# Seven half products for eight in eight pairs of projection blocks, with sums on VectorE and GpSimd and another step order

## What is computed

```python
proj = x @ w_in[l]
aq, ak, av, dqkv, dbeta, da, dz, gates = jnp.split(proj, SPLIT_POINTS, axis=-1)
...
dqkv = jax.nn.silu(causal_depthwise_conv(dqkv, conv_w[l]))
...
g = -jnp.exp(a_log[l].astype(jnp.float32)) * jax.nn.softplus(da.astype(jnp.float32) + dt_bias[l].astype(jnp.float32))
...
x = layer_norm(DEEPNORM_ALPHA * x + merged @ w_out[l], ln1_g[l], ln1_b[l])
h = jnp.square(jax.nn.relu(x @ w_up[l]))
x = layer_norm(DEEPNORM_ALPHA * x + h @ w_down[l], ln2_g[l], ln2_b[l])
```

## Time and profile before

| | us |
|---|---|
| median of 3 runs | 1449.0 |
| lowest, highest | 1446.56, 1449.88 |
| the profiled execution | 1448.78 |
| its span, as the profile has it | 1446.7 |
| TensorE busy | 1423.5 |
| VectorE busy | 893.3 |
| ScalarE busy | 525.6 |
| GpSimd busy | 316.0 |
| mean granted clock of TensorE | 0.996 of 2.4 GHz |

### The profile page before, as it was taken

One profiled execution on the slowest core, in us unless ns is written; L12 is line 12 of the kernel. 1 busy time (PEld: TensorE's weight loads), 2 busy tenths in 40 slices (PEclk: granted clock), 3 DMA queues, 4 the chain that ended last, 5 costly groups with the idle time before them and its releaser, 6 DMA issues.

```text
span 1446.7 us, 22466 instructions
## 1 busy us (share of the span) xinstructions
PE 1423.5 (98%) x8570; PEld 1173.8 (81%) x8570; DVE 893.3 (62%) x1710; ACT 525.6 (36%) x1182; POOL 316.0 (22%) x341
## 2 busy tenths in 40 slices
PE   8999999999999999999999999999999999999996
PEld 7888887888888888778888888888888788888885
DVE  3555323565656665455518798666764777777778
ACT  3221212333323333252302435555554544444540
POOL 3666534242422333133740000000000000000000
PEclk9999999999999999999999999999999999999998
DMA  6222524423443233134451234333444865555422
GB/s 221 73 87 101 167 97 129 122 73 98 125 110 109 72 107 89 63 107 148 172 206 58 88 131 166 139 140 146 160 161 165 330 215 185 165 169 182 127 70 117
DMA packets 114703, 194.92 MB, mean 135 GB/s; under 512 B 27760, under 2 KB 60592, under 8 KB 112304
## 3 DMA queue, kind: packets, MB, share of 16 engines
q1 hardware_dynamic: 105680, 174.21, 36.5%
q10 hardware_dynamic: 8928, 19.40, 3.6%
HBM read 135.84 MB, written 57.74 MB: 134 GB/s over the span
## 4 chain that ended last, share of the span: by engine, by line
PE 93%; DVE 4%; ACT 1%; DMA 1%; issue 0%; SPq 0%; ACTq 0%; DVEq 0%
PE ps L1819 15%; PE ps L1753 10%; PE ps L1754 10%; PE ps L1755 10%; PE ps L2189 6%; PE ps L2190 6%; PE ps L2191 6%; PE ps L2173 5%; PE ps L2172 5%; PE ps L2174 5%; PE ps L1887 4%; PE ps L1827 2%; PE ps L1968 1%; PE ps L1919 1%; PE ps L1765 1%; PE ps L1947 1%
## 5 line engine op out<-in xcount | busy, mean ns | idle before, releaser
L716 POOL TENSOR_TENSOR ring2l<-raw,ring2h 128x256 fp32r<-128x256 f32 x180 | 175.2, 1004 | 3.6
L2189 PE MATMUL ps<-thi,shi 128*128 128x512 f32 x416 | 162.5, 391 | 2.6 <-DVE tlow L1642 2.6
L2190 PE MATMUL ps<-tlow,shi 128*128 128x512 f32 x416 | 162.6, 391 | 0.0
L2191 PE MATMUL ps<-thi,slow 128*128 128x512 f32 x416 | 162.4, 390 | 0.0
L1819 PE MATMUL ps<-xh,ring2h 128*128 128x512 f32 x304 | 122.4, 403 | 0.0
L1819 PE MATMUL ps<-xl,ring2h 128*128 128x512 f32 x304 | 122.2, 402 | 0.0
L1819 PE MATMUL ps<-xh,ring2l 128*128 128x512 f32 x304 | 120.4, 396 | 0.0
L713 POOL CAST ring2h<-raw 128x1024 fp32r<-128x1024 f32 x45 | 48.8, 1085 | 322.5 <-PE ps L1819 177.2
L1753 PE MATMUL ps<-xh,ring2h 128*128 128x512 f32 x288 | 112.2, 390 | 0.0
L1754 PE MATMUL ps<-xl,ring2h 128*128 128x512 f32 x288 | 112.1, 389 | 0.0
L1755 PE MATMUL ps<-xh,ring2l 128*128 128x512 f32 x288 | 112.1, 389 | 0.0
(11 more groups left out here) (348 smaller groups left out, 3229.2 us busy)
## 6 DMA issues: line engine op xcount, KB each, us to landing
raw<-in_wblk SPq DMA_DIRECT2D x55, 512.0 KB, 3.3
sraw<-hpark SPq DMA_DIRECT2D x104, 256.0 KB, 2.8
hpark<-hq SPq DMA_DIRECT2D x16, 1024.0 KB, 4.6
b<-in_wblk SPq DMA_DIRECT2D x64, 256.0 KB, 3.5
wraw<-in_wblk SPq DMA_DIRECT2D x30, 512.0 KB, 4.0
park<-ub ACTq DMA_DIRECT2D x50, 256.0 KB, 2.0
hpark<-hq SPq DMA_DIRECT2D x16, 768.0 KB, 5.0
park<-cout ACTq DMA_DIRECT2D x12, 512.0 KB, 2.6
```

The lines of the kernel that those rows point to most:

```text
L716: ins = pool.tensor_tensor(lo[:, k:k + 2, :], src[:, k:k + 2, :], hi[:, k:k + 2, :].bitcast(F32), ALU.subtract)
L2189: mm(outp, shi[s][:, ts], thi[m][:, :], start=first, stop=False, skip_group_check=True)
L2190: mm(outp, shi[s][:, ts], tlow[m][:, :], start=False, stop=False, skip_group_check=True)
L2191: return mm(outp, slow[s][:, ts], thi[m][:, :], start=False, stop=final, skip_group_check=True)
```

## The change

Block 0 is now the first query block, and the 12 DeltaNet blocks are 1 to 12. Block 0 is projected as before. Blocks 1 to 16 are done as eight pairs: a pair (256 columns) and x are cut in quarters, A by rows of w and block, B by rows of w and token half. `in7` does seven products of half depth and 512 tokens, in the order P1, P5, P6, P2, P7, P3, P4, 12 matmuls each. P1, P6, P7 and P4 share one bank, P5 and P3 another, P2 has a third; between products ScalarE copies the bank's present state to cb (`in_snap`), and VectorE adds banks to these copies (`combine_in`). Two sets of four banks alternate.

- Four sums of x, T1 to T4, are made once, by VectorE, from the raw x, split by ScalarE and VectorE, and stored over the raw x and above.
- Four sums of weights for a pair, S1, S2, S4 and S3, are made by GpSimd (`in_sums`). High parts of the seven pieces are made by ScalarE (`in_hi`), low parts by VectorE (`in_lo`). Each piece has one buffer (A22 has two), so each waits for its product of the pair before.
- SP loads the two blocks of pair n when the raw data of pair n - 1 are used up: four sums and five low parts, for pair 1 all seven.
- ScalarE does the first tap of the convolution. The SiLU is done in place.
- The end of the decay chain is moved behind the last combination. The gate matmuls, block 17 and the split of blocks 17 and 18 on GpSimd follow the last pair.
- In the steps the order on all three engines and the list of fillers are others: 19 places for 14. TensorE's order is now: scores, kk, kq, t1, vn of the first chunk, y1, ds, pt, u1, ks of the second chunk, pv, y2, scores, vn of the second chunk, u2, ds, grow, y3, both o, u3, y4, u4, pt and trk, trq, ont, y5, pv, u5, trv, with fillers between.
- At the seam to the down projection the parts of step 2 come before ScalarE's relus and VectorE's four sums.
- For a single tile the inverse root takes seven instructions for nine.

All waits on shared semaphores are shifted by the counts of the new part. The core of the diff (without the orders of the steps on VectorE and ScalarE, which the text above and the functions' names tell, and the buffers' addresses):

```diff
+N_IP = 8
+I_SP, I_TX, I_SN, I_CS = 7 * N_IP, 4 * N_IP, 4 * N_IP, 3 * N_IP
+IPROD = [("A11", "B11", 0), ("S1", "T1", 1), ("S2", "T2", 0), ("A12", "B21", 2), ("S3", "T3", 0), ("S4", "B22", 1), ("A22", "T4", 0)]
...
+PREP0 = ("A11", "S1", "S2", "A12", "S3", "S4", "A22")
+PREP = ("A11", "A22", "S1", "S2", "A12", "S3", "S4")
...
+            def load_in(n):
+                sp.dma_start(raw[n % 2][:, :], A["wblk"][n, :, :]).then_inc(w_raw_in[n % 2], 16)
...
+            for n in range(1, N_IP + 1):
+                sp.wait_ge(tx_sum, 4 * n)
+                sp.wait_ge(up_w, 7 * n - 2 if n > 1 else 7)
+                load_in(2 * n + 1)
+                load_in(2 * n + 2)
...
+            def in_sums(n):
+                pool.wait_ge(w_raw_in[1], 16 * (n + 1))
+                pool.wait_ge(w_raw_in[0], 16 * (n + 2))
+                own = lambda k: ipw[k][2]
+                if n:
+                    pool.wait_ge(sp_mm, 7 * (n - 1) + I_P5)
+                pool.tensor_tensor(own("S1"), IA["A21"], IA["A22"], ALU.add).then_inc(tx_sum, 1)
+                pool.wait_ge(tx_sum, 4 * n + 1)
+                if n:
+                    pool.wait_ge(sp_mm, 7 * (n - 1) + I_P6)
+                else:
+                    pool.wait_ge(av_mm, NT)
+                pool.tensor_tensor(own("S2"), own("S1"), IA["A11"], ALU.subtract).then_inc(tx_sum, 1)
+                pool.wait_ge(tx_sum, 4 * n + 2)
+                if n:
+                    pool.wait_ge(up_w, 7 * (n - 1) + ip_order(n - 1).index("S4") + 1)
+                pool.tensor_tensor(s4raw, IA["A12"], own("S2"), ALU.subtract).then_inc(tx_sum, 1)
+                if n:
+                    pool.wait_ge(sp_mm, 7 * (n - 1) + I_P7)
+                pool.tensor_tensor(own("S3"), IA["A11"], IA["A21"], ALU.subtract).then_inc(tx_sum, 1)
+            for n in range(N_IP):
+                in_sums(n)
...
+            pool.wait_ge(sp_mm, 7 * (N_IP - 1) + I_P5)
+            pool.sem_inc(w_hi, 2 * N_IP)
+            pool.sem_inc(w_ready, 2 * N_IP)
+            split(N_IP, 1, ring2h[1], ring2l[1])
+            pool.wait_ge(sp_mm, 7 * N_IP)
+            split(N_IP + 1, 0, ring2h[0], ring2l[0])
+            split_ring(N_IP + 1, 1)
...
+            def in_hi(n, *pieces):
+                for k in pieces:
+                    hi, lo, src = ip_piece(n, k)
+                    assert ip_order(n)[ic["n"] % 7] == k
+                    ic["n"] += 1
+                    if k in ("A11", "A12"):
+                        act.wait_ge(w_raw_in[1], 16 * (n + 1))
+                    elif k == "A22":
+                        act.wait_ge(w_raw_in[0], 16 * (n + 2))
+                    else:
+                        act.wait_ge(tx_sum, 4 * n + {"S1": 1, "S2": 2, "S4": 3, "S3": 4}[k])
+                    if n == 0:
+                        if k == "A12":
+                            act.wait_ge(av_mm, NT)
+                        if k in ("S4", "A22"):
+                            act.wait_ge(uni_mm, 2)
+                    elif k == "A22":
+                        if n == 1:
+                            for h in range(2):
+                                act.wait_ge(ub_out[h], 16)
+                        else:
+                            act.wait_ge(sp_mm, 7 * (n - 2) + I_P4)
+                    else:
+                        act.wait_ge(sp_mm, 7 * (n - 1) + {"A11": I_P1, "S1": I_P5, "S2": I_P6, "A12": I_P2, "S3": I_P7, "S4": I_P3}[k])
+                    cp(hi, src).then_inc(up_hi, 1)
...
+            def t_hi(i):
+                act.wait_ge(ti_sum, 3 if i < 2 else 4)
+                cp(ith[IT_ORDER[i]][:, :, :, :], itr[IT_ORDER[i]][:, :, :, :]).then_inc(xh_ok, 1)
+            def in_snap(n, i):
+                prod, bank, block, half = ((I_P1, 0, 0, 0), (I_P5, 1, 1, 1), (I_P6, 0, 0, 1), (I_P4, 0, 1, 0))[i]
+                act.wait_ge(sp_mm, 7 * n + prod)
+                if n == 0:
+                    act.wait_ge(zero_ok, 2)
+                elif n >= 2:
+                    act.wait_ge(conv_ok, 2 * (n - 2) + block + 1)
+                if i == 3:
+                    act.wait_ge(cs_ok, 3 * n + 2)
+                cp(ip_cb(n, block, half), ip_bank(n, bank)).then_inc(snap_ok, 1)
...
+            def tap0(b):
+                n, p = divmod(b, 2)
+                act.wait_ge(cs_ok, 3 * n + 3)
+                act.wait_ge(snap_ok, 4 * n + 4)
+                if b == 0:
+                    act.wait_ge(c_in, 16 * 7)
+                if b >= 2:
+                    act.wait_ge(dn_out[p], 16 * n)
+                act.activation(cacc[p][:, :], cb[2 * (n % 2) + p][:, 0:S], ACT.Identity, bias=zero[:, 0:1], scale=convw[:, b, 0:1]).then_inc(tap_ok, 1)
+            def silu_store(b):
+                p = b % 2
+                act.wait_ge(conv_ok, b + 1)
+                act.activation(cacc[p][:, :], cacc[p][:, :], ACT.Silu).then_inc(silu_ok, 1)
...
+                act.dma_start(park[b, :, PAD:PAD + S], cacc[p][:, :]).then_inc(dn_out[p], 16)
...
+            in_hi(0, "A11", "S1")
+            t_hi(0)
+            in_hi(0, "S2")
+            t_hi(1)
+            in_hi(0, "A12")
+            q_half(0)
+            t_hi(2)
+            in_hi(0, "S3")
+            t_hi(3)
+            q_half(1)
+            in_hi(0, "S4", "A22")
+            for n in range(N_IP):
+                conv = 1 <= n <= N_DN // 2
+                ahead = n < N_IP - 1
+                if n:
+                    in_snap(n - 1, 3)
+                if conv:
+                    tap0(2 * n - 2)
+                    tap0(2 * n - 1)
+                if n == N_IP - 1:
+                    store_pair(n - 1)
+                in_snap(n, 0)
+                if ahead:
+                    in_hi(n + 1, "A11", "A22")
+                in_snap(n, 1)
+                if ahead:
+                    in_hi(n + 1, "S1")
+                if conv:
+                    silu_store(2 * n - 2)
+                in_snap(n, 2)
+                if ahead:
+                    in_hi(n + 1, "S2", "A12")
+                if conv:
+                    silu_store(2 * n - 1)
+                if ahead:
+                    in_hi(n + 1, "S3", "S4")
...
+            act.wait_ge(g_raw, 1)
+            act.activation(gtmp[:, 0, :, :], ba[:, :, 0:NH], ACT.Exp, scale=-1.0)
+            act.activation(gtmp[:, 5, 0, :], alog[:, :], ACT.Exp)
+            act.activation(gtmp[:, 2, :, :], gtmp[:, 2, :, :], ACT.Exp, scale=-1.0).then_inc(g_exp, 1)
+            in_snap(N_IP - 1, 3)
+            store_pair(N_IP - 1)
...
+            def conv(b):
+                p, src = b % 2, cb[b % 4]
+                dve.wait_ge(tap_ok, b + 1)
                 for k in range(1, 4):
...
+            ic = {"n": 0}
+            def in_lo(n, *pieces):
+                for k in pieces:
+                    hi, lo, src = ip_piece(n, k)
+                    assert ip_order(n)[ic["n"] % 7] == k
+                    ic["n"] += 1
+                    dve.wait_ge(up_hi, ic["n"])
+                    if k in ("S1", "S2"):
+                        dve.wait_ge(tx_sum, 4 * n + {"S1": 2, "S2": 3}[k])
+                    tt(lo, src, hi.bitcast(F32), ALU.subtract).then_inc(up_w, 1)
+            def combine_in(n, i):
+                prod, bank, block, half, snap = ((I_P2, 2, 0, 0, 1), (I_P7, 0, 1, 1, 2), (I_P3, 1, 0, 1, 3))[i]
+                dve.wait_ge(sp_mm, 7 * n + prod)
+                dve.wait_ge(snap_ok, 4 * n + snap)
+                c = ip_cb(n, block, half)
+                tt(c, c, ip_bank(n, bank), ALU.add).then_inc(cs_ok, 1)
+            def t_lo(i):
+                dve.wait_ge(xh_ok, NT + i + 1)
+                tt(itl[IT_ORDER[i]][:, :, :, :], itr[IT_ORDER[i]][:, :, :, :], ith[IT_ORDER[i]][:, :, :, :].bitcast(F32), ALU.subtract).then_inc(xl_ok, 1)
+            ti = {k: r[:, :, :, :] for k, r in itr.items()}
+            xq = lambda kk, half: xraw[:, 4 * half:4 * half + 4, 4 * kk:4 * kk + 4, :]
+            tt(ti["T3"], xq(1, 1), xq(0, 1), ALU.subtract).then_inc(ti_sum, 1)
+            tt(ti["T1"], xq(0, 1), xq(0, 0), ALU.subtract).then_inc(ti_sum, 1)
+            in_lo(0, "A11")
+            dve.wait_ge(ti_sum, 2)
+            tt(ti["T2"], xq(1, 1), ti["T1"], ALU.subtract).then_inc(ti_sum, 1)
+            dve.wait_ge(ti_sum, 3)
+            tt(ti["T4"], xq(1, 0), ti["T2"], ALU.subtract).then_inc(ti_sum, 1)
+            in_lo(0, "S1")
+            t_lo(0)
+            in_lo(0, "S2")
+            t_lo(1)
+            in_lo(0, "A12")
+            t_lo(2)
+            in_lo(0, "S3")
+            t_lo(3)
+            in_lo(0, "S4", "A22")
+            for n in range(N_IP):
+                convs = 1 <= n <= N_DN // 2
+                ahead = n < N_IP - 1
+                if convs:
+                    conv(2 * n - 2)
+                if ahead:
+                    in_lo(n + 1, "A11", "A22", "S1")
+                if convs:
+                    conv(2 * n - 1)
+                combine_in(n, 0)
+                if ahead:
+                    in_lo(n + 1, "S2", "A12")
+                combine_in(n, 1)
```

(59 more changed lines are left out.)

302 lines of the change are left out of this document (145 added, 157 removed).

## The result

The changed kernel takes 1468.7 us (median of 4 runs, 1467.2 to 1470.4) where the kernel before takes 1449.4 beside it: ratio 1.0135, 95% interval 1.0122 to 1.0149. That is 19.3 us more; the forecast was 11.1 more. The profiled execution has a span of 1466.1 us against 1446.7.

A forecast was written before the change was run, and what follows sets the result against it. TensorE, busy 98% of the span, was taken as the bound; -21.8 + 11.6 + 16.2 + 5.2 + 3.4 + 3.4 - 1.0 - 4.3 - 1.6 = +11.1 gave about 1460 us, range 1441 to 1473.

The forecast's parts named there:

- six pairs give nothing: Pairs after the first, with convolutions: 2.7 us stall before each seventh product, 21.8 us a pair as before; 16.2 us lost.
- a sum that meets VectorE costs it 1.2: Input projection: VectorE and GpSimd take turns by whole instructions, so a step meeting a 512-column sum waits 1.2 us.
- Faster: Rival, seventh product of each pair: GpSimd's sums fall where VectorE waits anyway, 0.5 us a pair; 1441 us, chance 22%.
- its own case: Whole kernel: the prediction's main forecast of 1452 to 1467 us, given a chance of 50%.
- The first pair: First of eight projection pairs: pauses of 2.8, 4.8 and 3.8 us before its second, third and fifth products; 11.6 us lost.
- 2 x 1.7 = 3.4: Slow clock behind the first pair's 3.8 us pause and the 5.2 us wait before the gate matmuls: 1.7 us each.
- I take two, 3.4: Slow clock behind the six 2.7 us pauses before seventh products: two of six charged, bounds 0 and 6 x 1.7.
- every pause drops the clock: Rival, waits before seventh products: each brings the slow clock, 4 x 1.7 us more; 1467, up to 1476; chance 15%.
- ends 0.2 + 0.7 + 7.0 after the sixth product: Seam to block 17: end of the decay chain, moved behind the last pair's combination 2; gate matmuls wait 5.2 us.
- The step order: Steps after the projection: the new order saves 1.0 us in all, between -3.6 and +1.6.
- The seam: Before the down projection: earlier lows of product 2 remove the pause and slow clock, 4.3 us less, bounds 3 and 4.3.
- The tail: Kernel's end: a shorter inverse root on VectorE for four tiles, 4 x 0.39 = 1.6 us less.

The follow-up runs named there:

- experiment 4: Changed kernel without GpSimd's 28 weight sums of pairs 1 to 7, whose products read other data of the same size: 1445.2 us, ratio 0.9978.
- experiment 9: Changed kernel with GpSimd's split of block 18 held back until the decay chain has ended: 1465.5 us, ratio 1.0119.
- experiment 5: Changed kernel with useless matmuls in TensorE's waits, nine before the seventh product of pairs 1 to 6, thirty before the gate matmuls: 1460.7 us, ratio 1.0086.

## Why the prediction was right, and where it was off

**The direction and its reason hold.** The turns are whole instructions (rows at 226.0, experiment 4), the wait stands before the seventh product and names VectorE's combination, and six pairs give nothing: 2.3 us of wait a pair where the forecast had 2.7. With the slow clock they cost 4.6 more than before. The step in which a sum that meets VectorE costs it 1.2 was right in kind: three sums a pair do, at 1.1 (S1, in five pairs on the low of A11, in one on that of A22), 1.1 (S4, on the low of S1) and 0.9 (S3, on the second convolution, in five pairs of six). The forecast had S4 beside the second convolution or behind it. The rival *Faster* would have needed the sums to fall into VectorE's waits; only that of S2 did.

**The size was partly luck.** 1468.7 lies above the 1452 to 1467 that the forecast called its own case, though inside its range of 1441 to 1473. Of its misses the waits of the first and of the six pairs were too high by 1.9 each, which hides a part of the 7.7 by which the clock was too low and the 2.0 of the gate matmuls.

**The first pair** has three waits of 3.7, 2.0 and 4.0 us, where the forecast had 2.8, 4.8 and 3.8, all three for the causes that it named. The third product starts at 50.66 instead of 49.3, mainly because two of VectorE's three small gate operations took 1.28 and 1.17 us beside GpSimd's first sums instead of the under 0.2 of the earlier trace rows. Its wait is only 2.0 because the second product, at the slow clock, ended 2.7 late. So the 9.7 against 11.6 is no sign that less was waited for: without that slow stretch it would be 12.4.

**The clock is the term that was mis-sized**: "2 x 1.7 = 3.4" and "I take two, 3.4" made 6.8, and 14.5 was measured. Block 17 had its 1.7 (1.9). In the six pairs a wait cost between 0.3 and 1.8, 6.6 in all: 1.6 to 1.8 in three pairs, about the price of the seam's row, and 0.3 to 0.6 in the others, though all but the first of these waits are 2.5 us long. In the first pair 6.0 us are lost. Behind the wait of 3.7, for which the forecast charged nothing, all twelve matmuls of the second product are slow, 2.7 us; this hides, as the third waits for ScalarE until 50.66 anyway. Behind the wait of 4.0 thirteen matmuls are slow (60.38 to 66.06), 2.7 us and not 1.7; some 0.6 is the rest of the three waits. Behind the wait that was forecast at 4.8 the clock is at full speed (the row at 50.96). The rival *every pause drops the clock* (1467) came nearest in time, but not in its rule: not every pause did.

**The decay chain**: "ends 0.2 + 0.7 + 7.0 after the sixth product" left out that GpSimd's split of block 18 starts at the seventh product's end and meets it. The forecast put that split under block 17, at no cost; experiment 9 prices it at 2.7 of wait. The chain alone is 6.5.

**Outside the projection** 4.9 us came, not 6.9. The step order gave nothing (46.19 and 46.20 us a step), inside its bounds of -3.6 and +1.6. The seam gave 4.0 of 4.3. The tail gave 1.1 of 1.6, since a step with a column as its scalar takes 0.22 us, not 0.16 (first and fourth step of one inverse root, and what follows it, in the changed kernel):

```profile
1441.15 0.15 DVE L1340 TENSOR_SCALAR lva<-bmv 128x1 f32<-128x1 f32 x1
...
1441.71 0.22 DVE L1330 SCALAR_TENSOR_TENSOR lnt<-lrs,lva 128x1 f32<-128x1 f32 x1
...
1442.80 1.29 DVE L1909 SCALAR_TENSOR_TENSOR zt<-zt,bmv,ln2gb 128x1024 f32<-128x1024 f32 x1
```

1.65 us where the earlier trace rows have 1.92.

What stays open is why a wait of 2.5 us drops the clock in some pairs and not in others. It isn't tied to the pair: in the changed kernel the pairs 3, 4 and 6 are slow (23.1 to 23.4 us against 21.8 and 22.1), in experiment 9, with the same order and the same waits there, the pairs 3, 5 and 6. No run here tells the cause.

## What to carry to other kernels

When an algorithm saves work on the engine that bounds the kernel and gives sums to two others, list for each product the one result that it waits for, and put that result at the head of its engine's queue: here the same work in another order was worth 40 us, the clock's share included. Price an instruction of VectorE whose operands are in SBUF, and that may meet one of GpSimd, at about its own time plus the other's remaining time, and place such pairs where nothing waits. Here a wait of TensorE of 2.5 us or more cost up to 1.8 to 2.7 us beyond its length: fill it, or count the slow clock behind it.

## What was not expected of the hardware

- Work of no use in a wait pays: 84 more matmuls made the kernel 7.1 us shorter (experiment 5), as the granted clock stayed at 1.00.
- A VectorE step of 0.19 us can last as long as the whole GpSimd instruction beside it (1.04); a chain of small dependent steps took 9.1 instead of 6.5 us beside 3.84 us of GpSimd work.
- A combination that reads one operand from PSUM did not take turns: at 93.21 it took 0.67 us, and the sum that GpSimd started inside it, at 93.55, its usual 1.29, while the low behind it, with both operands in SBUF, took 1.58. The Trainium skill, SBUF — State Buffer, section "Who interferes with whom", says so for an instruction with one SBUF input outside the faster modes; these rows agree.
